# One more plain step ahead of the steps with seven products, and the preparation for those steps put in pieces on VectorE

## What is computed

```python
h = rmsnorm(x, norm_ffn[i])
up = jnp.einsum("bsd,df->bsf", h, w_up)          # 1024 -> 2 x 2816
act, gate = up[..., :D_FF], up[..., D_FF:]
act = causal_dwconv(act, w_dw, b_dw)             # 3 taps over tokens
x = x + jnp.einsum("bsf,fd->bsd", jax.nn.silu(act) * gate, w_down)
```

## Time and profile before

| | us |
|---|---|
| median of 3 runs | 953.82 |
| lowest, highest | 953.04, 955.51 |
| the profiled execution | 952.04 |
| its span in the trace | 950.2 |

### The profile page before, as it was taken

One profiled execution on the slowest core, in us unless ns is written; L12 is line 12 of the kernel. 1 busy time (PEld: TensorE's weight loads), 2 busy tenths in 40 slices (PEclk: granted clock), 3 DMA queues, 4 the chain that ended last, 5 costly groups with the idle time before them and its releaser, 6 DMA issues.

```text
span 950.2 us, 14147 instructions
## 1 busy us (share of the span) xinstructions
PE 920.7 (97%) x5604; PEld 796.7 (84%) x5604; DVE 625.8 (66%) x833; ACT 438.0 (46%) x667; POOL 159.0 (17%) x114
## 2 busy tenths in 40 slices
PE   8999999999799999999999999888999999999997
PEld 7888898887689999988888898677989999888887
DVE  6999985679976666756343378996777766632333
ACT  7654476337354444563232374444554455522330
POOL 0565833001200000055000020040000001900000
PEclk9999999999999999999999999899999999999999
DMA  7233021222222332212322332212222232323212
GB/s 272 96 94 107 13 101 45 89 88 67 67 89 94 130 127 94 89 62 94 119 91 91 123 120 89 67 51 105 90 89 89 89 106 87 110 91 119 91 61 89
DMA packets 23193, 90.03 MB, mean 95 GB/s; under 512 B 3040, under 2 KB 6368, under 8 KB 20192
## 3 DMA queue, kind: packets, MB, share of 16 engines
q1 hardware_dynamic: 22560, 88.72, 27.5%
q10 hardware_dynamic: 576, 0.52, 0.2%
HBM read 86.09 MB, written 2.10 MB: 93 GB/s over the span
## 4 chain that ended last, share of the span: by engine, by line
PE 84%; DVE 10%; ACT 3%; issue 2%; POOL 1%; DVEq 0%; ACTq 0%; POOLq 0%
PE bank L1508 13%; PE bank L1510 12%; PE bank L1509 12%; PE bank L1821 6%; PE bank L1822 6%; PE bank L1823 6%; PE bank L1799 5%; PE bank L1801 5%; PE bank L1800 5%; PE bank L1550 2%; DVE w_lo L1042 2%; DVE u_lo L1280 2%; DVE mixed_whole L1300 1%; DVE as_is_whole L1291 1%; PE bank L1568 1%
## 5 line engine op out<-in xcount | busy, mean ns | idle before, releaser
L1509 PE MATMUL bank<-u_lo,w_hi 128*128 128x512 f32 (+1 forms) x374 | 140.9, 377 | 0.0
L1042 DVE TENSOR_TENSOR w_lo<-w_raw,w_hi 128x1408 fp32r<-128x1408 f32 (+2 forms) x49 | 90.0, 1836 | 68.3 <-ACT w_hi L614 67.5
L614 ACT ACTIVATE w_hi<-w_raw 128x1408 fp32r<-128x1408 f32 (+2 forms) x55 | 86.0, 1566 | 92.3 <-PE bank L1510 91.4
L486 POOL TENSOR_TENSOR u_lo<-u_sum,late_hi 128x512 fp32r<-128x512 f32 x32 | 52.1, 1666 | 344.6 <-ACT late_hi L908 344.6
L1508 PE MATMUL bank<-late_hi,w_hi 128*128 128x512 f32 (+1 forms) x272 | 102.6, 377 | 0.0
L1510 PE MATMUL bank<-late_hi,w_lo 128*128 128x512 f32 (+1 forms) x272 | 102.5, 377 | 0.0
L1821 PE MATMUL bank<-as_is,w_hi 128*128 128x512 f32 x256 | 101.0, 394 | 1.1 <-DVE w_lo L1343 1.1
L1822 PE MATMUL bank<-as_is,w_hi 128*128 128x512 f32 x256 | 100.8, 394 | 0.0
L1823 PE MATMUL bank<-as_is,w_lo 128*128 128x512 f32 x256 | 99.6, 389 | 0.0
L1508 PE MATMUL bank<-f_hi,w_hi 128*128 128x512 f32 x176 | 71.1, 404 | 14.4 <-DVE w_lo L1042 14.4
L867 ACT ACTIVATE ring_hi<-ring_sum 128x512 fp32r<-128x512 f32 x64 | 40.5, 632 | 93.4 <-DVE ring_sum L1317 56.9
(11 more groups left out here) (261 smaller groups left out, 2265.0 us busy)
## 6 DMA issues: line engine op xcount, KB each, us to landing
w_raw<-w_up SPq DMA_DIRECT2D x64, 512.0 KB, 4.5
w_raw<-w_down SPq DMA_DIRECT2D x32, 704.0 KB, 4.1
w_raw<-w_up SPq DMA_DIRECT2D x12, 1024.0 KB, 4.8
w_raw<-w_pw SPq DMA_DIRECT2D x11, 1024.0 KB, 5.5
x_res<-x SPq DMA_DIRECT2D x3, 512.0 KB, 6.8
out<-out_sb SPq DMA_DIRECT2D x12, 128.0 KB, 1.9
w_raw<-w_pw SPq DMA_DIRECT2D x4, 256.0 KB, 6.4
gathered<-stage SPq DMA_DIRECT2D x32, 32.0 KB, 2.1
```

The costliest lines, as they stand in the source:

```text
L614: nc.scalar.activation(w_hi[s][:, 0:columns], w_raw[s][:, 0:columns], ACT.Copy).then_inc(w_rounded[s], 1)
L1042: V.tensor_tensor(w_lo[s][:, 0:columns], w_raw[s][:, 0:columns], as_f32(w_hi[s][:, 0:columns]), SUB).then_inc(w_split[s], 1)
L1509: M.matmul(dst, a, lo, start=False, stop=False)
```

## The change

`PLAIN` goes from 3 to 4, so each layer has four plain steps and seven with seven products. `EARLY` stays 6: the result of the fourth plain step goes to `u_sum`, and `round_late` and `split_late` treat it with the other late ones. Three plain steps (`i < EARLY // 2`) have the u_hi and u_lo operations, the fourth has none.

The two `split_as_is` of a layer move from GpSimd's queue to VectorE's. The preparation stands at new places: `scale_h` in two parts of 2 and 6 operations, the `add_mixed`, `split_mixed` and `split_as_is` in pairs in the second and third plain step; `before_gate` holds what comes ahead of the multiplications by the factor and the gate, `behind_gate` what comes at the step's end. `split_unit(1, ...)` now comes ahead of the u_lo operations, and on ScalarE `round_unit(1, ...)` ahead of u_hi. `build_ahead` is dissolved: the same seven operations stand in the last plain step, the first sum ahead of the taps. The gate's low parts there come behind the multiplication by the gate.

```diff
-PLAIN = 3
+PLAIN = 4
...
-EARLY = 2 * PLAIN
+EARLY = 6
...
-            for n in range(2):
-                split_as_is(0, n)
             for c in range(LATE):
                 split_late(0, c)
...
+                if i == PLAIN - 1:
+                    round_op(layer, PLAIN, 0)
                 for t in range(2):
                     silu(layer, i, t)
                 if i == 1:
-                    for product in (5, 6, 7, 4):
-                        round_mixed(layer, product)
-                    for n in range(2):
-                        round_as_is(layer, n)
+                    round_as_is(layer, 1)
+                    round_mixed(layer, 5)
+                    round_mixed(layer, 6)
                 if i == PLAIN - 1:
-                    for n in range(4):
+                    for n in range(1, 4):
                         round_op(layer, PLAIN, n)
                     round_gate(layer, PLAIN, 0)
+                else:
+                    round_unit(1, m + i + 1, UNIT)
+                if i < EARLY // 2:
+                    for t in range(2):
+
+                        act.wait_ge(drained[2 + t], f + i + 1)
+                        nc.scalar.activation(u_hi[:, 2 * i + t, :], y[:, t, :], ACT.Copy).then_inc(u_rounded[t], 1)
+                if i == 0:
+                    round_as_is(layer, 0)
+                if i == 1:
+                    round_mixed(layer, 7)
+                    round_mixed(layer, 4)
+                if i == PLAIN - 1:
                     round_gate(layer, PLAIN, 1)
...
+                if EARLY + c < 2 * PLAIN:
+                    act.wait_ge(drained[2 + c % 2], DRAINED_UP[layer] + PLAIN)
+                else:
+                    act.wait_ge(gate_used[c % 2], step_of(layer, (EARLY + c) // 2) + 1)
...
-                    V.tensor_tensor(y[:, t, :], bank[2 + t][:, :], y[:, t, :], MUL).then_inc(drained[2 + t], 1)
...
+                    V.tensor_tensor(y[:, t, :] if i < EARLY // 2 else u_sum[:, 2 * i + t, :], bank[2 + t][:, :], y[:, t, :], MUL).then_inc(drained[2 + t], 1)
                 if i < PLAIN - 1:
                     split_unit(1, m + i + 1, UNIT)
+                else:
+                    split_gate(layer, PLAIN, 0)
+                for t in range(2 if i < EARLY // 2 else 0):
+                    dve.wait_ge(u_rounded[t], EARLY // 2 * layer + i + 1)
+                    V.tensor_tensor(u_lo[:, 2 * i + t, :], y[:, t, :], as_f32(u_hi[:, 2 * i + t, :]), SUB).then_inc(u_split[t], 1)
+                behind_gate(layer, i)
+
+            def before_gate(layer, i):
+
+                if i == 0:
+                    scale_h(layer, 0, 2)
                 if i == 1:
-                    for product in (7, 4):
-                        split_mixed(layer, product)
-
-            def scale_h(layer):
+                    add_mixed(layer, 5)
+                    add_mixed(layer, 6)
+                if i == 2:
+                    split_as_is(layer, 0)
+                if i == PLAIN - 1:
+                    add_weights(layer, PLAIN, 6)
+                    split_op(layer, PLAIN, 5)
+                    add_weights(layer, PLAIN, 3)
+                    split_op(layer, PLAIN, 6)
+                    split_op(layer, PLAIN, 3)
+
+            def behind_gate(layer, i):
+
+                if i == 0:
+                    scale_h(layer, 2, KD)
+                if i == 1:
+                    add_mixed(layer, 7)
+                    add_mixed(layer, 4)
+                    split_mixed(layer, 5)
+                    split_mixed(layer, 6)
+                if i == 2:
+                    split_as_is(layer, 1)
+                    split_mixed(layer, 7)
+                    split_mixed(layer, 4)
+                if i == PLAIN - 1:
+                    split_gate(layer, PLAIN, 1)
```

More of the change, by code:

```diff
@@ L1255, in plain_step @@
                     split_unit(0, m + i + 1, UNIT)
+                if i == PLAIN - 1:
+                    add_weights(layer, PLAIN, 5)
                 for t in range(2):
                     conv_rest(layer, i, t)
[L1258 to L1262, removed]
                 if i == PLAIN - 1:
-                    build_ahead(layer)
+                    split_op(layer, PLAIN, 1)
+                before_gate(layer, i)
                 for t in range(2):
@@ L1267, in plain_step @@
                     V.tensor_tensor(y[:, t, :], y[:, t, :], rms[:, :], MUL).then_inc(act_scaled[t], 1)
-                if i == 1:
-                    for product in (5, 6):
-                        split_mixed(layer, product)
-                if i == PLAIN - 1:
-                    for half in range(2):
-                        split_gate(layer, PLAIN, half)
                 for t in range(2):
@@ L1276, in plain_step @@
                     dve.wait_ge(unit_done[1], m + i + 1)
-                    V.tensor_tensor(y[:, t, :], bank[2 + t][:, :], y[:, t, :], MUL).then_inc(drained[2 + t], 1)
-                for t in range(2):
-                    dve.wait_ge(u_rounded[t], PLAIN * layer + i + 1)
-                    V.tensor_tensor(u_lo[:, 2 * i + t, :], y[:, t, :], as_f32(u_hi[:, 2 * i + t, :]), SUB).then_inc(u_split[t], 1)
+                    V.tensor_tensor(y[:, t, :] if i < EARLY // 2 else u_sum[:, 2 * i + t, :], bank[2 + t][:, :], y[:, t, :], MUL).then_inc(drained[2 + t], 1)
@@ L1289, in scale_h, with split_as_is @@
+            def scale_h(layer, first, last):
                 norm = "ffn0" if layer == 0 else "ffn1"
-                for c in range(KD):
+                for c in range(first, last):
                     V.scalar_tensor_tensor(as_is_whole[c // KH][:, :, 1, c % KH, :], x_res[:, c, :].rearrange("p (h t) -> p h t", h=2), col(norm, c), rms[:, :].rearrange("p (h t) -> p h t", h=2), MUL, MUL).then_inc(h_scaled, 1)
+            def split_as_is(layer, n):
+                dve.wait_ge(as_is_rounded, 2 * layer + n + 1)
+                dve.wait_ge(mixed_added, 4 * (layer + 1))
+                V.tensor_tensor(as_is[n][:, :, 1, :, :], as_is_whole[n][:, :, 1, :, :], as_f32(as_is[n][:, :, 0, :, :]), SUB).then_inc(as_is_split, 1)
@@ L1297, in add_mixed @@
                 dve.wait_ge(h_scaled, KD * (layer + 1))
-                dve.wait_ge(mixed_added, 4 * layer + MIXED[product]) if layer or MIXED[product] else None
+                if layer or MIXED[product]:
+                    dve.wait_ge(mixed_added, 4 * layer + MIXED[product])
                 a, b = {5: (near[1], near[0]), 6: (far[1], whole[0]), 7: (far[1], near[1]), 4: (far[0], whole[1])}[product]
```

26 lines of the change are left out of this document (3 added, 23 removed).

## The result

The changed kernel takes 929.41 us (median of 4 runs, 928.98 to 930.74); the kernel before took 954.16 us beside it (4 runs, 953.04 to 955.51). The ratio is 0.9742, 95% interval 0.9726 to 0.9759: faster by 2.4 to 2.7%. The profiled run took 928.98 us, its span is 927.2 us; the forecast for it was 929.4 and 927.6.

A forecast was written before the change was run, and what follows sets the result against it. TensorE, busy 97%, was taken as the bound, with its gaps and lower clock to win. Layer savings of 10.25 and 12.35 us gave 22.6, so the median falls from 953.82 to 931.2 us; range 929.0 to 937.0.

The forecast's parts named there:

- What bounds the kernel: Whole span: TensorE is busy for 97%, so time can come only from its gaps, its clock or its work.
- the sum: Both up-projection stretches: 10.25 us less in layer 0, 12.35 in layer 1, together 22.6; span 950.2 to 927.6.
- One step more is plain: Fourth step of each layer: 21.76 us stand where 21.08 stood, +0.68 us a layer, +1.36 in all.
- First plain step: Slot 1's split starts at 209.8 behind two scalings; 4 us to spare in layer 0, 2.0 in layer 1.
- Second and third plain step: Slot 1's splits end at 232.5 and 253.5; as_is costs VectorE 4.6 us a layer, replacing 6.9 standing still.
- Loads: Last three half loads for the entry land at about 260.2, first sum due at 261.4: hidden by 1.2 us.
- Entry: First products of seven: copy has 1.1 us to spare; gate weights' split costs 0.2 us wait per layer, bounds 0 to 1.1.
- (b): First step of seven products stays late: copy and gate low parts wait as before, 936 us; chance 0.10.
- (d): Change does little: late units move instead of going, two waits of 4 to 5 us a layer, 950 to 953; chance 0.03.
- (c): A plain unit of each layer still late, most likely layer 1's, 2 to 5 us and lower clock, 934 to 940; chance 0.09.
- (e): Slower: VectorE, put at 67.5 of 87.0 us, bounds the plain steps and makes every unit late, say 956; chance 0.02.
- The median: Whole kernel: 931.2 us forecast from 953.82, the profiled run at 929.4 taken as 1.8 us under it.

## Why the prediction held

**What bounds the kernel.** Right. TensorE's gaps and its spells at the lower clock were what there was to take. The 22.93 us of the stretches are the 22.6 of the sum, which was 0.15 and 0.18 short in the two layers, mostly because the gate wait of 0.2 us did not come.

**One step more is plain,** +0.68 us a layer: the stretch of a plain step is 21.76 us, the first step of seven products 21.12. But the sum took the fourth step as the price of the entry. The runs show it as one way among others: three plain steps with the pieces placed well leave no wait over 0.3 us either. The 0.68 us are real in the stretches (1.18 and 0.98 us for the pair of layers, forecast 1.36), and half of that comes back at the end of the kernel. The forecast had no such term.

**First plain step.** Right to 0.1 us: the split was forecast from 209.8 (the whole run lies 0.4 us later) and started at 210.21; forecast to spare in layer 1 2.0 us, measured 2.1.

**Second and third plain step.** u_lo falls to 1.29 us, as_is takes 2.29 us as the row of the same shape said, and 232.5 and 253.5, the forecast ends of the splits, are 232.8 and 254.0. That u_lo had been held by GpSimd was inferred from two ends that were said to coincide. They don't quite: as_is ends at 242.98 (233.03 and 9.95) and u_lo at 243.54 (235.31 and 8.23), 0.56 us later. That is nearly the 0.69 us of one u_lo, as it must be if the second one runs when GpSimd's instruction has ended. The run with as_is on VectorE and the one with GpSimd's pieces show that the cause was right.

**Loads.** Hidden, as forecast: the first sum starts at 261.78 us, forecast 261.4.

**Entry.** Better than forecast by 0.2 us a layer. The split of the gate's first half ends at about 273.9 (272.73 and half of 2.35), as forecast with the 0.4 us added. The term that was mis-sized is the need: I took the weight load to start 0.3 us ahead of the first gate matmul, and it starts 0.06 us ahead of it, so the split was just in time. The load, then the matmul, which follows the one before it by the usual 0.12 us:

```profile
274.07 0.19 PEld L1843 LDWEIGHTS bank<-as_is,w_hi 128*128 128x128 f32 x1
```

```profile
274.01 0.28 PE L1823 MATMUL bank<-mixed,ring_lo 128*128 128x256 f32 x1
274.13 0.44 PE L1843 MATMUL bank<-as_is,w_hi 128*128 128x512 f32 x1
```

**Rivals.** (b), a late entry, is what as_is on VectorE does with three plain steps. (d), 950 to 953 us, has the time of either part alone: 950.8 us for the fourth plain step, where the waits simply stay, and 950.3 for as_is, where they move on as (d) says. (c) is seen in the run with all scalings ahead, at the place that was named (layer 1, first plain step) and costs 2.0 us. (e), VectorE as the bound, shows nowhere: in the three last plain steps of the changed kernel it is busy for 59.94 of 65.3 us (61.57 in layer 1) and TensorE never waits. It was nearer than the forecast had it, though: over the four plain steps VectorE was put at 67.5 of 87.0 us and is busy for 74.68 and 78.88. The forecast counted five weight splits where layer 0 has seven, and left out the norm's work (a reciprocal of 3.35 us alone). The rule of the Trainium skill about moving work off a saturated VectorE (Perfetto Trace Analysis, "Optimizing Scalar/DVE Operations") does not hold here, and the section's own warning about these two engines does: with as_is on GpSimd VectorE loses 7.6 us, with as_is itself 4.6.

**The median.** I added 1.8 us to the profiled run's forecast, the distance of before. The changed kernel's profiled run lies 0.4 under its median. That is 1.4 of the 1.8 us between 931.2 and 929.4; the other 0.4 is the span, 23.0 us shorter where 22.6 were forecast. With that the range held the measured 929.41 by little: it lies 0.4 us above the low end, 929.0.

## What to carry to other kernels

When TensorE waits for another engine's queue, list for every piece of that queue when it is due, and put work without a near due time behind work with one; here 10.4 us of 24.7 came from order, added as the last of three parts. A repaired stall lets the consumer reach the next one earlier, so edits have to be tried together as well as alone: the same move was worth 3.8 us without room at the entry and 10.95 with it. Before giving GpSimd an operation "because it is idle", compare what VectorE would need for it with what VectorE loses beside it: here 4.6 against 6.9 to 7.6 us, and still 5.6 with GpSimd's work in eight pieces.

## What the runs showed of the hardware

**VectorE beside GpSimd.** VectorE's operations whose two tensors lie in SBUF stand still until the running GpSimd instruction ends: w_lo 5.50 instead of 2.29 us beside 128x2048 instructions of some 5.6 us, 3.37 beside 128x512 instructions of 1.9 us in the mean. Those with one operand in a PSUM bank do not (act_in, 1.28 us for two, in both). The three-operand form y<-act_in,par,y is held as well (1.47 instead of 0.75 us). The Trainium skill's page SBUF — State Buffer, section "SBUF: two separate sides", says that the two engines share a port pair which is locked for a whole instruction by whichever starts first, while the other blocks. The trace agrees in all of these rows, and in both directions: with as_is back on GpSimd the first mixed subtraction starts at 237.03, ahead of GpSimd's 237.07, and keeps its 1.23 us while GpSimd's first instruction takes 5.66; the second, at 238.17, takes 5.64. GpSimd's two take 11.22 us there, 9.95 before.

**The clock after a wait.** Waits of the same length did not always cost the same. Behind a wait of 2.3 us in the same place the granted clock of the next 2.6 us was 1.00 in the kernel before and in the one with GpSimd's pieces, and 0.51, 0.65 and 0.62 in the runs with four plain steps, with four and as_is moved, and with three and as_is moved. These are means: in the run with four and as_is moved TensorE started again at 220.84 and the clock was 1.00 until 221.6, then 0.50. Stretches of that run, the first behind the 2.33 us wait and the second behind the one of 4.35 (length, busy PE, PEld, DVE, ACT, POOL; PEclk; DMA share, GB/s):

```profile
220.80:223.40 2.60, 2.56 (x8) 2.09 (x9) 2.60 (x3) 1.52 (x2) 0.00 (x0) 0.65 0.64 183
...
604.40:607.00 2.60, 2.58 (x6) 2.12 (x7) 2.60 (x3) 1.52 (x2) 0.00 (x0) 0.50 0.65 192
```

Behind 1.75 us, and behind 2.34 us with as_is back on GpSimd, it stayed at 1.00; behind 3.5 us it was 0.54 and 0.57, and behind every wait of over 4 us 0.50 to 0.53. What decides between the two levels behind 2.3 us was not found. The clock is most of why removing waits paid more than their length: 3.7 of the 4.1 us that the stretches won beyond the 7.0 of waits.
